# Second attention stage: values' copies ahead of a unit of weights, weights behind the keys' copies, gate row and values' differences at later steps

## The chip, the cores and the metric

The kernel runs on one core of one Trainium2 chip. The time is the device time of one execution in microseconds (us); a kernel's time is the median over its runs. Of the kernel before there are three: 981.32, 981.45 and 982.88 us, median 981.45. One more execution was profiled, and the trace is of that one: it took 983.12 us, of which 981.3 lie between its first and last instruction.

## The reference

Two transformer blocks over 512 tokens of width 1024, all in float32. The first joins a multi-scale pooling branch and a "forgetting" attention. The change lies in the attention of the second block:

```python
h = rmsnorm_2(x, g_norm1[l]) * (1.0 + sc1) + sh1
proj = h @ w_in[l]
q_sb, k_sb, v_sb, q_ca, k_ca, v_ca = jnp.split(proj, split_pts, axis=-1)
o_sb = stick_breaking_attention(hs(q_sb, N_SB_HEADS), hs(k_sb, N_SB_HEADS), hs(v_sb, N_SB_HEADS))
q_ca = rmsnorm_2(hs(q_ca, N_CA_HEADS), g_q[l])
k_ca = rmsnorm_2(hs(k_ca, N_CA_HEADS), g_k[l])
o_ca = chunked_relpos_attention(q_ca, k_ca, hs(v_ca, N_CA_HEADS), rel_bias[l])
mixed = jnp.concatenate([o_sb.reshape(B, S, D_SB), o_ca.reshape(B, S, D_CA)], axis=-1)
x = x + gt1 * (mixed @ w_o[l])
```

`gt1` (the first gate) is a row of 1024 numbers that is needed only in the last line above. Each of the two kinds of attention has 8 heads of width 64.

## The kernel before, in words

Each float32 product is made of three matmuls (lines 2092 to 2094): every factor is split into an upper half in a reduced format (a copy by ScalarE, `wh`, `hh`, `ah`) and the rest (a subtraction by VectorE, `wl`, `hl`, `al`). The weights come in units of 1 MB, loaded by SyncE (line 549) into three buffers `raw`; a load waits until VectorE has taken the last piece of the unit that lay there before (`dve_wl`). ScalarE makes `wh` of it (line 698), VectorE `wl` (line 1237).

The second block's attention is a program of 188 steps. A step is one group of three matmuls of a projection or of the output product; beside it, by a table of numbers (`PACE_S`), stand "beats" of the attention: a score of head h and row block i (S, line 2238), a transposition of the weights of attention (T, line 2259), a product with the values (V, lines 2288 and 2291). Each engine has the same steps written in its own order, and semaphores tie them together. Steps 0 to 63 are the chunked attention's queries and keys, four pairs of heads (pairs 4 to 7); steps 64 to 95 the values of the stick-breaking attention in four row blocks; steps 96 to 159 its queries and keys (pairs 8 to 11); then comes the output product. A pair's heads are 2p and 2p+1: head 8 is scored first at step 33, head 10 at step 49, head 18 at step 137, head 20 at step 154.

SyncE's queue carries, in the order of a loop over m (16 steps each):

- `twice(p)` (line 580): four copies inside SBUF that put a pair's keys, upper and lower half, on the other 64 partitions too, 128 KB each; the first score of the pair waits for all four (`dma_kd0` or `dma_kd1`);
- `table(h)` (line 608): a head's table of position biases, 256 KB;
- the units of weights (line 549), 1 MB;
- for the stick-breaking values: ScalarE writes block i of the values into `values_at(i)` (buffers `rows` and `v_end`, line 1084, at steps 78, 79, 91, 95); `values_out(i)` (line 614) writes it to DRAM as `value_rows`, in two DMAs with runs of 64 numbers (256 bytes); `values_before(i)` (line 624) reads the same rows back, shifted down by one token, into `dv[i]` (named `x` or `sgt` in the trace); a first row of zeros is written by line 648.

VectorE takes the difference of neighbouring values, `dv[i]` less values, at the steps in `DV` (line 1732). ScalarE copies the result's upper half into `v_sb` one step later (`DV_UPPER`, line 1092), VectorE writes the lower half (`DV_LOWER`, line 1736). Nothing reads `v_sb` before step 134 (head 16).

GpSimd's queue has memsets in the tables (line 2045), and between those of heads 9 and 10 the first gate: `gate_rows()` (line 1995) writes the gate from `mod` to DRAM number by number, in two DMAs of 2 KB, and `gate(0)` (line 2002) waits for them and reads the row back to all 128 partitions, 512 KB, into `gt`. It is used by line 1755 from 611.5 us on. After the tables GpSimd clears parts of `v_rows` and `strip` (lines 2057 to 2059) and then waits for the end of the attention.

```python
def score(h, i):
    ...
                else:
                    e.wait_ge(d[f"kd{p % 2}"], 64 * (p // 2) - 64)
```

Of the kernel before, what the change touches and what calls it, by code (L numbers as in the profile page):

```python
# [18 lines left out]
NR, NH = 3, 2  # L19
# [110 lines left out]
def program(nc, x, xcols, wall, wf, poolw, params, fng, wada, crow_in, rel, out):  # L130
# [32 lines left out]
    with ExitStack() as ctx:  # L163
# [331 lines left out]
        TURN_BANK_2 = ((1, 0), (4, 5))  # L495
        VSB_OUT = (78, 79, 91, 95)

        DV, DV_UPPER, DV_LOWER = (87, 88, 113, 122), (88, 89, 114, 123), (89, 90, 115, 124)
        VSB_BANK, W_O_BANK = (0, 1, 2, 0), ((1, 0, 4, 5), (2, 3, 6, 7))

        def o_step(n):
# [43 lines left out]
        def _(e):  # L545
# [5 lines left out]
            def loads_to(last):  # L551
                while todo[0] <= min(last, W_MLP + 3):
                    n = todo[0]
                    todo[0] += 1
                    if n >= NR:
                        e.wait_ge(v["wl"], 4 * (n - NR) + 4)
                    load(n, place[n])
# [52 lines left out]
            def values_out(i):  # L610

                e.wait_ge(a["vsb"], i + 1)
                for odd in range(2):
                    e.dma_start(heads_of(v_mem[1 + 128 * i:129 + 128 * i, :])[:, :, odd, :],
                                values_at(i)[:, :, odd, :]).then_inc(d[f"vm{i % 2}"], 16)
# [14 lines left out]
            for m in range(10):  # L630
                if 1 <= m < 5:
                    twice(3 + m)
                for b_ in range(first_s[16 * m], first_s[16 * m + 16]):
                    x_ = beats_s[b_]
                    if x_ and x_[0] == "S" and x_[2] == 0 and x_[1] + 2 in CA:
                        table(x_[1] + 2)
                if m == 5:
                    values_out(2)
                    values_out(3)
                    values_before(2)  # L640
                    values_before(3)
                loads_to(W_CA + m + 1 + NR)
                if m == 4:
                    for j in range(4):
                        e.wait_ge(d[f"x{4 + j}"], 32)

                    e.wait_ge(g["strip"], 1)
                    e.dma_start(v_mem[0:1, :], dv[0][0:1, :]).then_inc(d["vm0"], 16)
                    values_out(0)
                    values_out(1)  # L650
                    values_before(0)
                    values_before(1)
                if m >= 6:
                    twice(2 + m)
            loads_to(W_O + 1 + NR)
# [1285 lines left out]
        def _(e):  # L1941
# [49 lines left out]
            def gate_rows():  # L1991

                e.wait_ge(v["mod"], 1)
                for c in (0, 4):
                    e.dma_start(gates[0, 128 * c:128 * c + 512].rearrange("(c p) -> p c", p=128),
                                mod[:, 16 + c:20 + c], allow_slow_non_contiguous=True).then_inc(d["g0"], 16)
# [46 lines left out]
            for h in CA:  # L2043
                e.wait_ge(d[f"bt{h % 2}"], 16 * (h // 2 - 3))
                e.memset(bt[h % 2][0:64, 448:512], NEG).then_inc(g["bt"], 1)
                if h == 9:
                    for j in range(4):
                        e.wait_ge(d[f"x{4 + j}"], 32)
                    e.wait_ge(v["tile"], 48)
                    e.memset(dv[0][0:1, :], 0.0).then_inc(g["strip"], 1)  # L2050
                    gate_rows()
                    gate(0)

            e.wait_ge(v["qn"], 8)
            e.wait_ge(v["tile"], 40)
# [1 line left out]
                e.memset(v_rows[i][:, :, 64:128], 0.0).then_inc(g["strip"], 1)  # L2057
            e.memset(strip[:, 0:384], 0.0).then_inc(g["strip"], 1)
            e.tensor_scalar(strip[:, 384:512], ident[:, :], 1.0, None, ALU.mult).then_inc(g["strip"], 1)
            e.wait_ge(t["value"], n_turn(23, 0))  # L2060
            for i in range(4):
                r = sm[:, 144 + i:145 + i]
# [625 lines left out]
```

## Time and profile before

| | |
|---|---|
| median of 3 runs | 981.45 us (981.32, 981.45, 982.88) |
| the profiled execution | 983.12 us |
| its span, first to last instruction | 981.3 us |
| TensorE matmul busy | 959.3 us (98%) |
| VectorE, ScalarE, GpSimd busy | 686.3, 538.6, 83.2 us |
| DMA | 148.69 MB, mean 152 GB/s |
| granted TensorE clock, mean | 0.998 |

A row names the line of the kernel, the engine, the operation with out<-in and the shape, how often it stands there and its time; behind it the engine's idle time and what ended it. A time in us from the start of the span stands in front in the views by time. PE is TensorE, DVE VectorE, ACT ScalarE, POOL GpSimd, SPq SyncE's queue. "DMA to landing" is the time from the issue of a DMA until its data is there.

### The profile page before, as it was taken

The page shows a single profiled execution, that of the slowest core. Times are in us where ns is not written, and L with a number is a line of the kernel's source. Part 1 is how long each engine was busy: PE and PEld are TensorE (multiplying, and loading weights), DVE is VectorE, ACT ScalarE, POOL GpSimd, SP SyncE. Part 2 cuts the span into 40 slices and gives each one's busy share as a digit, 9 for nine tenths or more (in the row PEclk, how much of TensorE's full clock was granted, in tenths as well). Part 3 has the DMA queues.
Part 4 walks back from the last instruction along what each step waited for, and adds up shares of the span by engine and source line. Part 5 has one row for each costly group of instructions (what it writes and reads, how often), then busy time and mean ns, then how long its engine had stood idle before and what let it go on. Part 6 is the DMA issues. An engine that isn't in the chain of part 4 may idle for free.

```text
span 981.3 us, 13125 instructions
## 1 busy us (share of the span) xinstructions
PE 959.3 (98%) x4712; PEld 800.2 (82%) x4712; DVE 686.3 (70%) x1269; ACT 538.6 (55%) x1053; POOL 83.2 (8%) x173
## 2 busy tenths in 40 slices
PE   8999999999999999999989999999999999999998
PEld 7878998878888888777777887788888888888886
DVE  6487888868788759767668886966644853774773
ACT  6448777753223345489877563446645634644520
POOL 4000001011122012100000000110000001000000
PEclk9999999999999999999999999999999999999999
DMA  8205222238787425644433323446777567473201
GB/s 298 82 24 185 66 76 87 81 145 335 298 318 281 173 108 188 241 92 154 111 119 92 102 65 136 158 112 153 180 221 178 171 201 191 115 224 129 85 33 54
DMA packets 36673, 148.69 MB, mean 152 GB/s; under 512 B 9193, under 2 KB 9193, under 8 KB 24706
## 3 DMA queue, kind: packets, MB, share of 16 engines
q1 hardware_dynamic: 23970, 101.41, 29.6%
q0 software_dynamic: 9568, 42.48, 16.5%
q10 hardware_dynamic: 3072, 3.98, 1.2%
q8 instruction: 38, 0.62, 0.3%
q14 instruction: 25, 0.20, 0.1%
HBM read 138.32 MB, written 5.27 MB: 146 GB/s over the span
## 4 chain that ended last, share of the span: by engine, by line
PE 81%; DVE 9%; ACT 4%; DMA 3%; issue 2%; POOL 0%; SPq 0%; ACTq 0%; DVEq 0%; POOLq 0%
PE psum L2092 24%; PE psum L2094 24%; PE psum L2093 24%; PE psum L2259 3%; PE psum L2238 2%; PE psum L2288 1%; DVE wl L1237 1%; PE psum L2291 1%; DMA raw<-in_wall 1%; DVE two L1776 1%; DMA value_rows<-rows 1%; DVE hl L1277 1%; DVE two L1641 1%; DMA al<-al 1%; DVE xt L1273 1%
## 5 line engine op out<-in xcount | busy, mean ns | idle before, releaser
L2092 PE MATMUL psum<-hh,wh 128*128 128x512 f32 (+1 forms) x720 | 274.2, 381 | 0.7 <-DVE hl L1277 0.6
L2094 PE MATMUL psum<-hh,wl 128*128 128x512 f32 (+1 forms) x720 | 267.4, 371 | 0.0
L2093 PE MATMUL psum<-hl,wh 128*128 128x512 f32 (+1 forms) x720 | 267.4, 371 | 0.0
L1237 DVE TENSOR_TENSOR wl<-raw,wh 128x512 fp32r<-128x512 f32 x328 | 213.8, 683 | 45.6 <-ACT wh L698 45.3
L698 ACT ACTIVATE wh<-raw 128x512 fp32r<-128x512 f32 x328 | 188.8, 620 | 84.1 <-PE psum L2094 68.2
L2092 PEld LDWEIGHTS psum<-hh,wh 128*128 128x128 f32 x720 | 135.4, 188 | 24.3 <-DVE hl L1277 1.5
L2094 PEld LDWEIGHTS psum<-hh,wl 128*128 128x128 f32 x720 | 135.3, 188 | 23.7
L2093 PEld LDWEIGHTS psum<-hl,wh 128*128 128x128 f32 x720 | 135.6, 188 | 21.1 <-issue 1.0
L2092 PE MATMUL psum<-wh,ah 128*128 128x512 f32 x224 | 88.5, 395 | 0.0
L2094 PE MATMUL psum<-wh,al 128*128 128x512 f32 x224 | 87.4, 390 | 0.0
L2093 PE MATMUL psum<-wl,ah 128*128 128x512 f32 x224 | 87.3, 390 | 0.0
L857 ACT ACTIVATE pth<-psum 128x128 fp32r<-128x128 f32 (+4 forms) x104 | 45.9, 442 | 16.4 <-PE psum L2259 15.3
L2259 PE MATMUL psum<-ident,p_sb 128*128 128x128 f32 x272 | 47.2, 276 | 7.2 <-DVE ptl L1449 6.8
L1154 ACT ACTIVATE two<-psum 128x512 f32<-128x512 f32 x32 | 19.1, 598 | 62.2 <-PE psum L2094 62.1
L1449 DVE TENSOR_TENSOR ptl<-psum,pth 128x128 fp32r<-128x128 f32 (+1 forms) x96 | 46.2, 482 | 7.4 <-ACT pth L857 6.8
L2092 PEld LDWEIGHTS psum<-wh,ah 128*128 128x128 f32 x224 | 42.1, 188 | 9.2 <-issue 0.6
L2094 PEld LDWEIGHTS psum<-wh,al 128*128 128x128 f32 x224 | 42.1, 188 | 8.9
L2259 PEld LDWEIGHTS psum<-ident,p_sb 128*128 128x128 f32 x272 | 33.5, 141 | 18.7 <-issue 9.3
L2093 PEld LDWEIGHTS psum<-wl,ah 128*128 128x128 f32 x224 | 42.1, 188 | 8.0
L832 ACT ACTIVATE p_sb<-p_sb,sm 128x528 f32<-128x528 f32 (+3 forms) x64 | 36.0, 563 | 9.5 <-DVE sm L1424 8.1
L838 ACT ACTIVATE p_sb<-p_sb,sm 128x528 f32<-128x528 f32 (+3 forms) x64 | 35.7, 558 | 1.5 <-DVE sm L1429 1.4
L2092 PE MATMUL psum<-wh,hh 128*128 128x512 f32 x76 | 31.6, 416 | 1.2 <-DVE wl L1237 1.2
(335 smaller groups left out, 1632.5 us busy)
## 6 DMA issues: line engine op xcount, KB each, us to landing
raw<-in_wall SPq DMA_DIRECT2D x78, 1024.0 KB, 5.1
raw<-in_wall POOLq DMA_DIRECT2D x15, 1024.0 KB, 7.9
wa<-in_wada POOLq DMA_DIRECT2D x24, 512.0 KB, 6.1
gt<-in_wada POOLq DMA_DIRECT2D x20, 512.0 KB, 6.1
xt<-in_xcols SPq DMA_DIRECT2D x8, 264.0 KB, 8.2
cb<-c_rows SPq DMA_DIRECT2D x8, 264.0 KB, 3.2
x<-in_x SPq DMA_DIRECT2D x4, 512.0 KB, 10.1
x_kept<-x SPq DMA_DIRECT2D x4, 512.0 KB, 2.8
```

Of the source, the lines that this page charges most:

```text
L698: e.activation(home(w)[0][:, 512 * c:512 * c + 512], raw_of(w, c), ACT.Copy).then_inc(a["wh"], 1)
L832: e.activation(block_p(h, i), block_p(h, i), ACT.Exp, bias=nmx, scale=1.0 if h in FG else -1.0, accum_out=su).then_inc(a["exp"], 1)
L838: e.activation(block_p(h, i), block_p(h, i), ACT.Copy, scale=mx).then_inc(a["norm"], 1)
L857: e.activation(ph[0:rows, PT[j]:PT[j] + w_], bank[bk][0:rows, 0:w_], ACT.Copy).then_inc(a["turn"], 1)
L1154: e.activation(two[:, n % 2, :], bank[w1_bank(n)], ACT.Relu).then_inc(a["r"], 1)
L1237: e.tensor_tensor(home(w)[1][:, cs], raw_of(w, c), home(w)[0][:, cs].bitcast(F32), ALU.subtract).then_inc(v["wl"], 1)
L1449: e.tensor_tensor(dst, bank[bk][0:rows, 0:w_], ph[0:rows, o:o + w_].bitcast(F32), ALU.subtract).then_inc(v["turn"], 1)
L2092: e.matmul(out_, lh, rh, start=start, stop=False, skip_group_check=True)
L2093: e.matmul(out_, lh, rl, start=False, stop=False, skip_group_check=True)
L2094: return e.matmul(out_, ll, rh, start=False, stop=stop, skip_group_check=True)
L2238: ins = e.matmul(dst[:, size * j:size * j + size], q[:, 128 * i:128 * i + 128], k[:, size * j:size * j + size], start=k is k_up, stop=k is ...
L2259: ins = e.transpose(bank[bk][:, 128 * (i - i0):128 * (i - i0) + 128], head(h)[0][:, o:o + 128], ident[:, :])
```

## The change

```diff
@@ the steps of the values' differences
-        DV, DV_UPPER, DV_LOWER = (87, 88, 113, 122), (88, 89, 114, 123), (89, 90, 115, 124)
+        DV, DV_UPPER, DV_LOWER = (90, 92, 113, 122), (91, 93, 114, 123), (92, 94, 115, 124)
@@ SyncE, in the loop over m
-                loads_to(W_CA + m + 1 + NR)
-                if m == 4:
+                if m == 3:
                     for j in range(4):
                         e.wait_ge(d[f"x{4 + j}"], 32)
 
                     e.wait_ge(g["strip"], 1)
                     e.dma_start(v_mem[0:1, :], dv[0][0:1, :]).then_inc(d["vm0"], 16)
+                if m == 4:
                     values_out(0)
                     values_out(1)
                     values_before(0)
                     values_before(1)
+                if 1 <= m < 5:
+
+                    e.wait_ge(d[f"kd{(3 + m) % 2}"], 64 * ((3 + m) // 2) - 64)
+                loads_to(W_CA + m + 1 + NR)
                 if m >= 6:
                     twice(2 + m)
@@ GpSimd, behind the table of head 9
                     e.memset(dv[0][0:1, :], 0.0).then_inc(g["strip"], 1)
-                    gate_rows()
-                    gate(0)
...
             e.tensor_scalar(strip[:, 384:512], ident[:, :], 1.0, None, ALU.mult).then_inc(g["strip"], 1)
+            e.wait_ge(t["pq"], 12)
+            gate_rows()
+            gate(0)
```

For m from 1 to 4 the unit of weights is now issued only when the pair's four copies have landed, and for m = 4 behind the values' DMAs too. The first gate's three DMAs stand behind GpSimd's last memsets and wait for `pe_pq` 12, the end of step 127.

No instruction is added or removed on an engine. SyncE's queue around m = 4 (L549 is a unit of weights, L580 the keys' copies, L608 a table, L614 and L624 the values to DRAM and back), before:

```order
L580 DMA al<-al 64x512 [waits dve_kl] x2
L608 DMA sgt<-in_rel 128x512 [waits dve_score] x2
L549 DMA raw<-in_wall 128x2048 [waits dve_wl]
L648 DMA value_rows<-x 1x512 [waits dma_x7,dma_x6,pool_strip,dma_x5,dma_x4]
L614 DMA value_rows<-rows 512x1x64 [waits act_vsb]
L614 DMA value_rows<-rows 512x1x64
L614 DMA value_rows<-rows 512x1x64 [waits act_vsb]
L614 DMA value_rows<-rows 512x1x64
L624 DMA x<-value_rows 128x512 [waits dma_vm0]
L624 DMA x<-value_rows 128x512 [waits dma_vm1]
L608 DMA sgt<-in_rel 128x512 [waits dve_score]
```

The same place in the changed kernel:

```order
L580 DMA al<-al 64x512 [waits dve_kl] x2
L608 DMA sgt<-in_rel 128x512 [waits dve_score] x2
L614 DMA value_rows<-rows 512x1x64 [waits act_vsb]
L614 DMA value_rows<-rows 512x1x64
L614 DMA value_rows<-rows 512x1x64 [waits act_vsb]
L614 DMA value_rows<-rows 512x1x64
L624 DMA x<-value_rows 128x512 [waits dma_vm0]
L624 DMA x<-value_rows 128x512 [waits dma_vm1]
L549 DMA raw<-in_wall 128x2048 [waits dve_wl,dma_kd1]
L608 DMA sgt<-in_rel 128x512 [waits dve_score]
```

The unit went from ahead of the values' six DMAs to behind them, with a wait for `dma_kd1`; the row of zeros (L648) moved up to m = 3.

VectorE from step 87 on (L1732 the differences, L1736 their lower halves, L1417 a score's logits, L1449 the lower half of a transposition, L1457 a head's output, L1237 `wl`), before:

```order
L1449 TENSOR_TENSOR ptl<-psum,pth 128x512 [waits act_turn]
L1429 RECIPROCAL sm<-sm 128x1 [waits act_exp] x2
L1732 TENSOR_TENSOR x<-x,rows 128x512 [waits dma_dv0,act_vsb]
L1732 TENSOR_TENSOR x<-x,rows 128x512 [waits dma_dv1,act_vsb]
L1457 TENSOR_TENSOR tmp<-psum,tmp 64x512 [waits dve_ol,act_o]
L1736 TENSOR_TENSOR v_sb<-x,v_sb 128x8x64 [waits act_dv]
L1417 ISA p_sb,sm<-psum,sgt 128x512 [waits pe_turn,pool_bt,pe_score]
L1417 ISA sm 128x1
L1449 TENSOR_TENSOR ptl<-psum,pth 128x128 [waits act_turn]
L1736 TENSOR_TENSOR v_sb<-x,v_sb 128x8x64 [waits act_dv]
L1237 TENSOR_TENSOR wl<-raw,wh 128x512 [waits act_wh]
```

The same place in the changed kernel, whose lines stand four further down (L1736 and L1740 are the differences and their lower halves, L1421, L1453, L1461 and L1241 the rest):

```order
L1461 TENSOR_TENSOR tmp<-psum,tmp 64x512 [waits dve_ol,act_o]
L1421 ISA p_sb,sm<-psum,sgt 128x512 [waits pe_turn,pool_bt,pe_score]
L1421 ISA sm 128x1
L1453 TENSOR_TENSOR ptl<-psum,pth 128x128 [waits act_turn]
L1736 TENSOR_TENSOR x<-x,rows 128x512 [waits dma_dv0,act_vsb]
L1241 TENSOR_TENSOR wl<-raw,wh 128x512 [waits act_wh]
L1421 ISA p_sb,sm<-psum,sgt 128x384 [waits pe_score]
L1421 ISA sm 128x1
L1453 TENSOR_TENSOR ptl<-psum,pth 128x256 [waits act_turn]
L1736 TENSOR_TENSOR x<-x,rows 128x512 [waits dma_dv1,act_vsb]
L1740 TENSOR_TENSOR v_sb<-x,v_sb 128x8x64 [waits act_dv]
L1241 TENSOR_TENSOR wl<-raw,wh 128x512 [waits act_wh]
```

The two differences, which wait for DMAs, stood ahead of head 12's output, head 14's first logits and head 13's first transposition; now these three come first.

## Rows read from the trace of the kernel before

**Rows 1.** Waits of TensorE from 400 to 540 us: total, times, longest

```profile
PE psum L2259 <- DVE ptl L1449: 3.9, 3, 3.0
...
PE psum L2092 <- DVE wl L1237: 1.2, 2, 0.7
```

**Rows 2.** TensorE in order of time: start, us, what, [idle before]

```profile
426.06 0.47 PE L2238 MATMUL psum<-k_sb,q_sb 128*128 128x512 f32 x1 [0.69 <-DMA low<-low]
...
445.89 0.47 PE L2238 MATMUL psum<-ah 128*128 128x512 f32 x1 [1.39 <-DMA al<-al]
...
497.59 0.87 PE L2259 MATMUL psum<-ident,p_sb 128*128 128x128 f32 x3 [3.00 <-DVE ptl L1449]
...
546.15 0.62 PE L2238 MATMUL psum<-v_ca 128*128 128x512 f32 x2
...
566.26 0.47 PE L2238 MATMUL psum<-k_sb,q_sb 128*128 128x512 f32 x1
```

**Rows 3.** Stretches: length, busy PE, PEld, DVE, ACT, POOL, PEclk, DMA share, GB/s

```profile
440.00:480.00 40.00, 37.40 (x187) 29.56 (x186) 29.97 (x82) 36.06 (x86) 0.44 (x3) 1.00 0.39 118
...
494.50:497.50 3.00, 0.09 (x1) 0.00 (x0) 2.75 (x7) 2.58 (x7) 1.96 (x7) 1.00 0.04 14
497.50:501.00 3.50, 3.41 (x10) 2.86 (x11) 3.50 (x9) 3.08 (x8) 0.37 (x1) 0.51 0.31 70
```

**Rows 4.** The chain of waits from 485 to 500 us: start, us, what

```profile
484.77 6.55 DMA value_rows<-rows
...
491.33 3.32 DMA x<-value_rows
```

**Rows 5.** VectorE in order of time

```profile
492.99 0.69 DVE L1732 TENSOR_TENSOR x<-x,rows 128x512 f32<-128x512 f32 x1 [4.16 <-DMA x<-value_rows]
494.75 0.69 DVE L1732 TENSOR_TENSOR x<-x,rows 128x512 f32<-128x512 f32 x1 [1.07 <-DMA x<-value_rows]
```

**Rows 6.** SyncE's queue in order of time

```profile
479.59 0.44 SPq L549 DMA_DIRECT2D raw<-in_wall  x1
480.50 5.37 SPq L614 DMA_DIRECT2D value_rows<-rows  x4
490.22 1.44 SPq L624 DMA_DIRECT2D x<-value_rows  x2
...
536.56 5.38 SPq L580 DMA_DIRECT2D v_ca<-v_ca  x4
...
556.04 1.26 SPq L580 DMA_DIRECT2D low<-low  x2
```

**Rows 7.** Landings: unit of 479.59; value_rows from 484.0; value_rows from 503.3

```profile
DMA to landing us min/median/max: 9.1/9.1/9.1
...
DMA to landing us min/median/max: 4.7/5.6/6.5
...
DMA to landing us min/median/max: 2.1/2.2/2.2
```

**Rows 8.** Landings of keys' copies: from 474.4; 440.6; 421.0 to 423.3; 541.5; from 556.0

```profile
DMA to landing us min/median/max: 2.2/2.2/2.2
...
DMA to landing us min/median/max: 5.0/5.0/5.0
...
DMA to landing us min/median/max: 2.5/2.8/3.6
...
DMA to landing us min/median/max: 2.8/2.8/2.8
...
DMA to landing us min/median/max: 5.6/5.7/5.7
```

**Rows 9.** GpSimd in order of time; last row: landings of L1995's two DMAs

```profile
425.36 0.76 POOL L1995 DMA_DIRECT2D gate_rows<-mod  x1 [7.81 <-issue]
437.85 0.56 POOL L2002 DMA_DIRECT2D gt<-gate_rows  x1 [11.73 <-DMA gate_rows<-mod]
...
DMA to landing us min/median/max: 8.3/10.2/12.2
```

## The prediction

> **What bounds the kernel now.** The table of the page comes first: TensorE's matmuls fill 98% of the span, so only what makes TensorE wait, or run slowly, costs time. Next, the waits of TensorE around the change [rows 1]: between 400 and 540 us it waits 3.9 us for VectorE's lower halves of transpositions, 3.0 of it at once, and 1.2 us for `wl`. TensorE in order of time [rows 2] adds two waits for keys' copies, 0.69 us at 426.06 (head 8's first score) and 1.39 us at 445.89 (head 10's), and places the 3.00 us before 497.59. Then the stretches [rows 3]: in the stretch from 494.5 to 497.5 TensorE is busy 0.09 us, and in the next one, to 501, its granted clock is 0.51, the lower of its two levels (1.2 instead of 2.4 GHz). So TensorE stood still for 3.00 us and then did 3.5 x (1 - 0.51) = 1.7 us less than it could have.
>
> Why does VectorE come late? Its own rows [rows 5]: it stood 4.16 us before the first difference of values (492.99) and 1.07 us before the second (494.75). The transposition that TensorE wanted is behind them in VectorE's order. The chain of waits [rows 4] goes on: the readback behind the second difference took 3.32 us, and before it a write of `value_rows` issued at 484.77 took 6.55 us. In SyncE's queue [rows 6] a 1 MB unit of weights was issued at 479.59, right ahead of the values' writes from 480.50 on. The unit took 9.1 us to land and the writes from 484.0 on 4.7 to 6.5 us; writes of the same kind from 503.3 on, with no unit ahead, took 2.1 to 2.2 us [rows 7].
>
> **The change part by part.** Terms are us of the profiled execution, 983.12 us.
>
> *Values: unit behind them, differences three and four steps later.* Two remedies for one stall. With writes of 2.2 us instead of 6.5, the second block's write, issued at 484.77, lands at 487.0 and not 491.3, its readback (3.32) at 490.3, and the first block's before that. The later place gives more: VectorE, idle from 488.8 until the data came [rows 5], first does head 12's output and head 14's logits, which follow TensorE to step 90. TensorE came to step 91's transposition at 494.59 (497.59 less 3.00, [rows 2]), so it leaves step 90 near 493.5, and the second difference, two steps on, is not wanted before 495. The data are there by 488.7 and 490.3, or, had the landings not improved at all, at 493.0 and 494.7, about when they are wanted. Gain: the 3.00 us, and with them the slow stretch, 1.7 us, since no idle TensorE precedes it: **-4.7**. If VectorE still comes late by a little, the slow stretch goes and some wait stays; bounds -4.7 and 0.
>
> The skill's page "TensorE: Matmul & The Clock Gate" (the Trainium skill, section on the HAM clock gate) says that an idle TensorE falls to half rate, and that the place at which the rate changes varies from run to run. The trace agrees with the first: 3.00 us idle, then 0.51 [rows 3]. By the second, some executions of the kernel before would be spared the 1.7 us.
>
> The times fit that, and this is where I chose. Three runs are 981.32, 981.45 and 982.88, the profiled one 983.12: two values near 981.4 and two near 983.0, apart by 1.6, the price of the slow stretch. I take the median to be executions with the 3.00 us wait but without the slow stretch, and forecast the changed kernel from the profiled execution, whose waits I can see. Against the median the gain is 1.7 us smaller than the sum.
>
> *Cost of the later place.* Four instructions of some 0.6 us each (two differences, 0.69 by their rows, two lower halves of the same shape) enter VectorE's steps 90 to 94, where `wl` of unit 36 and head 14's logits also stand. The same instructions ran before in a row behind the stall, so the work is no more; but in steps 90 to 95 VectorE has little spare time. Nothing reads `v_sb` before step 134, so only what is queued behind matters: `wl`, wanted from step 96, and transpositions. A delay of one such instruction on TensorE, 0.6, is the upper end, nothing the lower; I take **+0.4**. ScalarE's copies (one step behind each difference) move with them at the same count.
>
> *Units behind the keys' copies (m = 1 to 4), gate away from 417 to 443 us.* The copy that head 10's score waited for was issued at 440.6 and took 5.0 us; in the same time ran the gate row's broadcast (issued 437.85 [rows 9]), and behind the copy in SyncE's queue two tables and a unit. Copies with nothing beside them took 2.2 us [rows 8]. The tables stay, the others go: landing before 444, while TensorE was ready at 444.5. The wait of 1.39 goes; ScalarE, busy 36.06 of the next 40 us [rows 3], can follow only as far as it had idle time itself, so I take **-1.2** (bounds -1.39 and 0, if the tables alone delay the copy). For head 8 the last copy took 2.5 of the pair's 2.5 to 3.6 us; at 2.2 it lands 0.3 earlier: **-0.3** (0 to -0.69). The price is that the units come later: by 2 to 3 us for m = 1 to 3, by about 9 for m = 4 (issued near 488). The unit of m = 4 is number 38, which ScalarE first reads at step 113, over 20 steps later, and the others lie as far off, so they cost nothing; for a unit wanted within 5 us of its landing the delay would count in full.
>
> *The gate at its new place.* GpSimd waits for the end of step 127, ten steps ahead of head 18's score at 546.15 [rows 2], so near 535. From there it is 8.6 us to the second write (7.81 + 0.76), 12.5 to the broadcast (425.36 to 437.85, [rows 9]), and about 5 to its landing, so until 561. The row is used from 611.5 on, and GpSimd has nothing queued behind it before that. But it now runs beside the copies of pairs 9 and 10. Pair 9's last copy is issued at 541.5, lands 2.8 later at 544.3 [rows 8] and is wanted at 546.15 [rows 2]: 1.85 us to spare. Pair 8's predecessor at the old place, pair 4, ran beside the gate's writes and took up to 3.6 instead of 2.2, so 1.4 more [rows 8]: still in time. Pair 10's last copies (issue 556.7, 5.7 to land, 562.4) are wanted at 566.26: 3.9 to spare, against some 3 us that a 512 KB broadcast beside them can add (440.6's copy: 5.0 less 2.2). I take **0**, bounds 0 and +1.5.
>
> Sum: -4.7 + 0.4 - 1.2 - 0.3 + 0 = -5.8, with 0.2 for what the 1.2 us of `wl` waits may lose when neighbours move: **-6.0**. 983.12 - 6.0 = **977.1 us**, 4.3 below the median of 981.45. All bounds on the good side give 976.3.
>
> **The rivals.** "Faster" below means more than 0.2% (2.0 us), about what a measurement of this kernel can tell from no change: below 979.5.
>
> *A, part of the wait stays.* VectorE is crowded in steps 90 to 95: behind the stall it was busy 2.75 + 3.50 of 6.5 us [rows 3], to which the first difference, 0.6, is now added. For it: TensorE already waits 1.2 us for `wl` [rows 1]. Against: `wl` is first wanted at step 96, and before the stall VectorE had idle time. It leaves 1.0 to 3.0 of the 3.00 us: 978.1 to 980.1; if the whole wait came back with its slow stretch, 981.8.
>
> *B, the stall was not the copies'.* If the values' small runs (256 bytes) and not the unit make the writes slow, the landings stay at 4.7 to 6.5. Against: the same runs took 2.1 to 2.2 us without a unit. Even then the later steps hide nearly all; waits of 0.5 to 1 us stay: 978.
>
> *C, slower.* The gate's writes delay the keys' copies of pair 9. Price: the gate's own second write took 12.2 us [rows 9]. If the last copy did, it would land at 553.7, and TensorE would wait 7.5 us at 546.15 and then run at the lower clock for another 1.7: 977.1 + 9.2 = 986.3. It decides from a landing over 4.7 us (546.15 - 541.5), and makes the kernel slower than 983.4 (the median and 0.2%) from 9.3 us on (9.3 - 4.65 + 1.7 = 6.3). Against it: 1.4 us was all that the same writes did to pair 4's copies. The Trainium skill's page "DMA: Bandwidth & Descriptors" (Queues, rings and completion order) says that a DMA engine serves its queues in turn, a packet at a time; by that rule GpSimd's small writes would slow SyncE's copies by a share and not hold them for 12 us, but would also slow them wherever the gate is put.
>
> **How the numbers follow.** Forecast (976.0 to 978.2): 0.64. A: 0.18, two thirds of it below 979.5. B, or a small wait at pairs 9 or 10 (978 to 979): 0.08. No measurable change, from a cause that I don't see or from A's full return: 0.06. C: 0.04. Faster 0.64 + 0.12 + 0.08 + 0.02 = 0.86, same 0.10, slower 0.04. The range goes from 975.6 (all bounds, and the `wl` waits gone) to 979.8.
>
> **What would show it.** VectorE: no wait for `value_rows` readbacks, or under 0.5 us. TensorE: no wait of 3.0 us near 491 to 495, and granted clock 1.00 in every stretch. No wait for a copy at heads 8 and 10 over 0.4 us. The values' first writes land in about 2.2 to 3 us. The gate's broadcast lands near 555, and heads 18 and 20 don't wait. A TensorE wait for VectorE of over 1 us in steps 91 to 100 speaks for A, one for a DMA at head 18 or 20 for C. Wrong altogether: the stall goes and the span stays.

## The result, and the profile after

The changed kernel is slower.

| | before | after |
|---|---|---|
| median | 981.38 us (980.17 to 982.88, 4 runs) | 988.31 us (987.84 to 988.78, 4 runs) |
| ratio, 95% interval | | 1.0077 [1.0056, 1.0098] |
| the profiled execution, its span | 983.12, 981.3 us | 988.78, 987.0 us |
| granted TensorE clock, mean | 0.998 | 0.995 |
| forecast | | 977.1 us, range 975.6 to 979.8 |

The measured time lies 8.5 us above the range. In the changed kernel's lines the score's matmuls are L2243, transpositions L2264, lower halves of transpositions L1453, `wl` L1241, the gate's writes L1999 and its broadcast L2006.

First the waits of TensorE, here from 400 to 620 us (total, times, longest), to be held against [rows 1]:

```profile
PE psum L2243 <- DMA v_ca<-v_ca: 11.1, 1, 11.1
PE psum L2264 <- DVE ptl L1453: 2.0, 4, 0.7
PE psum L2097 <- DVE wl L1241: 1.2, 2, 0.7
PE psum L2243 <- DMA low<-low: 0.5, 1, 0.5
```

What was to go is gone: the wait of 3.00 us for `ptl` and the one for `al` (1.39), and head 8's copy costs 0.50 in place of 0.69. At the top stands a new one of 11.1 us, for a copy of keys (L2243 reads them; the program's name for that buffer is `v_ca`). TensorE in order of time places it at head 18's first score, 546.15 before [rows 2]:

```profile
550.70 1.19 PE L2243 MATMUL psum<-v_ca 128*128 128x512 f32 x2 [11.08 <-DMA v_ca<-v_ca]
551.68 0.63 PE L2097 MATMUL psum<-hh,wh 128*128 128x512 f32 x1
552.11 0.63 PE L2098 MATMUL psum<-hl,wh 128*128 128x512 f32 x1
```

Without the wait that score would have stood at 539.62, and before it stood at 546.15: up to there the changed kernel is 6.5 us ahead, and then loses 11.1. The matmuls behind the wait take 0.63 us instead of 0.39. The stretches (length, busy PE, PEld, DVE, ACT, POOL, granted clock, DMA share, GB/s) say why:

```profile
480.00:500.00 20.00, 20.00 (x108) 16.98 (x107) 14.53 (x43) 17.35 (x45) 2.43 (x8) 1.00 0.55 149
...
530.00:532.00 2.00, 1.67 (x12) 1.25 (x10) 1.63 (x4) 1.98 (x6) 0.00 (x0) 1.00 2.36 66
532.00:534.00 2.00, 2.00 (x15) 1.74 (x14) 2.00 (x4) 1.36 (x5) 0.00 (x0) 1.00 0.55 29
...
540.00:542.00 2.00, 0.00 (x0) 0.00 (x0) 0.95 (x3) 0.00 (x0) 0.00 (x0) 1.00 0.86 357
542.00:544.00 2.00, 0.00 (x0) 0.00 (x0) 0.00 (x0) 0.00 (x0) 0.00 (x0) 0.89 1.02 233
...
550.00:552.00 2.00, 1.30 (x3) 1.15 (x4) 0.00 (x0) 0.08 (x1) 0.56 (x1) 0.50 0.21 16
552.00:554.00 2.00, 2.00 (x8) 1.57 (x8) 1.23 (x1) 0.89 (x2) 0.00 (x0) 0.55 0.77 229
```

From 480 to 500, where the stall was, TensorE is busy the whole time at clock 1.00. At head 18 it idles from 539.6 on; the clock falls to 0.50, the lower level, and is still there when the work starts again: 1.3 x 0.50 + 2.0 x 0.45 = about 1.5 us lost.

The DMA column is the second thing to see there: between 530 and 540 the engines are occupied (a packet's time and bytes are counted in the stretch in which it starts, so a share can be over 1), but next to nothing moves; the bytes come from 540 on. What stands in the queues at that time, SyncE's and then GpSimd's, in order of time:

```profile
529.46 0.33 SPq L549 DMA_DIRECT2D raw<-in_wall  x1
529.84 5.38 SPq L580 DMA_DIRECT2D v_ca<-v_ca  x4
```

```profile
528.15 0.85 POOL L1999 DMA_DIRECT2D gate_rows<-mod  x1 [33.53 <-PE psum L2099]
537.96 0.77 POOL L1999 DMA_DIRECT2D gate_rows<-mod  x1 [8.96 <-issue]
550.57 0.56 POOL L2006 DMA_DIRECT2D gt<-gate_rows  x1 [11.85 <-DMA gate_rows<-mod]
```

The gate's first write goes out 1.3 us ahead of a 1 MB unit of weights and 1.7 to 6.6 us ahead of the four copies of pair 9. Their landings, in this order: the unit of 529.46, the copy of 534.76, the gate's two writes:

```profile
DMA to landing us min/median/max: 13.9/13.9/13.9
...
DMA to landing us min/median/max: 15.7/15.7/15.7
...
DMA to landing us min/median/max: 9.4/10.9/12.3
```

Before, the same unit took 5.5 us and the last copy 2.8 [rows 8]. The chain of waits has it as one link: `534.76 15.69 DMA v_ca<-v_ca`. The queues' packets between 529 and 540 us show what kind of slowness it is (packets, MB, share of 16 engines' time):

```profile
q1 hardware_dynamic: 42, 0.34, 90.0%
q0 software_dynamic: 32, 0.00, 1.7%
```

q1 is SyncE's queue: 42 packets in 11 us, 0.90 x 11 x 16 / 42 = 3.8 us each. They are the unit's, 8 KB each (0.34 MB / 42). The experiment with the gate elsewhere (the late gate, below) has the same unit's packets, 8 KB each too, from 529 to 533.8 us:

```profile
q1 hardware_dynamic: 122, 1.00, 64.7%
```

That is 0.647 x 4.8 x 16 / 122 = 0.41 us each. So the unit did not wait behind one long transfer; each of its packets took some nine times as long. q0 is GpSimd's queue: its 32 packets, the gate's first write, took 0.09 us each, and all of them started before 530.4.

The rest of the change, in SyncE's queue, did what it was to do (before: [rows 6]); the last row here is the landing of the four writes:

```profile
478.44 4.78 SPq L614 DMA_DIRECT2D value_rows<-rows  x4
483.27 1.95 SPq L624 DMA_DIRECT2D x<-value_rows  x2
...
DMA to landing us min/median/max: 2.1/2.2/2.3
```

The writes land in 2.1 to 2.3 us instead of up to 6.5, the readbacks are issued at 483.3 instead of 490.2, and VectorE waits for no readback.

So the account of the profiled executions is -6.5 up to head 18, +11.1, +1.5: +6.1, where the spans differ by 5.7. Two questions were left: is the gate's new place alone the cause, and what about it holds the copies?

### The profile page after: what moved, and what is told of

Read it like the earlier page. It is cut to its first block, busy times and chain, and to the rows that moved or that the text cites. A ratio compares the mean times of both kernels' runs of the same rounds, so it can differ in the third digit from the quotient of the medians.

```text
span 987.0 us, 13130 instructions
## 1 busy us (share of the span) xinstructions
PE 959.4 (97%) x4712; PEld 800.4 (81%) x4712; DVE 686.3 (70%) x1269; ACT 538.2 (55%) x1053; POOL 83.2 (8%) x173
## 4 chain that ended last, share of the span: by engine, by line
PE 82%; DVE 9%; ACT 4%; DMA 3%; issue 2%; POOL 0%; ACTq 0%; DVEq 0%; SPq 0%; POOLq 0%
PE psum L2097 24%; PE psum L2099 24%; PE psum L2098 24%; PE psum L2264 3%; PE psum L2243 2%; DMA v_ca<-v_ca 2%; PE psum L2293 1%; PE psum L2296 1%; DVE wl L1241 1%; DMA raw<-in_wall 1%; DVE two L1780 1%; ACT wh L702 1%; DVE hl L1281 1%; DVE two L1645 1%; DVE xt L1277 0%
## 5 line engine op out<-in xcount | busy, mean ns | idle before, releaser
L1241 DVE TENSOR_TENSOR wl<-raw,wh 128x512 fp32r<-128x512 f32 x328 | 214.1, 685 | 45.6 <-ACT wh L702 45.2
L861 ACT ACTIVATE pth<-psum 128x128 fp32r<-128x128 f32 (+4 forms) x104 | 46.1, 444 | 16.2 <-PE psum L2264 15.1
L1453 DVE TENSOR_TENSOR ptl<-psum,pth 128x128 fp32r<-128x128 f32 (+1 forms) x96 | 46.3, 483 | 7.6 <-ACT pth L861 7.1
L2264 PE MATMUL psum<-ident,p_sb 128*128 128x128 f32 x272 | 47.0, 275 | 4.0 <-DVE ptl L1453 3.8
L2264 PEld LDWEIGHTS psum<-ident,p_sb 128*128 128x128 f32 x272 | 33.6, 141 | 15.3 <-issue 5.9
L1442 DVE TENSOR_TENSOR_SCAN p_sb<-p_sb,rows 128x512 f32<-128x512 f32 (+3 forms) x32 | 26.1, 818 | 13.1 <-ACT p_sb L848 13.0
## 6 DMA issues: line engine op xcount, KB each, us to landing
wa<-in_wada POOLq DMA_DIRECT2D x24, 512.0 KB, 5.8
gt<-in_wada POOLq DMA_DIRECT2D x20, 512.0 KB, 7.0
x<-in_x SPq DMA_DIRECT2D x4, 512.0 KB, 10.2
x_kept<-x SPq DMA_DIRECT2D x4, 512.0 KB, 2.8
```

The costliest lines, as they stand in the source:

```text
L861: e.activation(ph[0:rows, PT[j]:PT[j] + w_], bank[bk][0:rows, 0:w_], ACT.Copy).then_inc(a["turn"], 1)
L1241: e.tensor_tensor(home(w)[1][:, cs], raw_of(w, c), home(w)[0][:, cs].bitcast(F32), ALU.subtract).then_inc(v["wl"], 1)
L1442: e.tensor_tensor_scan(p[:, ::-1], p[:, ::-1], ends_at[:, ::-1], 0.0, ALU.mult, ALU.add).then_inc(v["scan_s"], 1)
L1453: e.tensor_tensor(dst, bank[bk][0:rows, 0:w_], ph[0:rows, o:o + w_].bitcast(F32), ALU.subtract).then_inc(v["turn"], 1)
L2264: ins = e.transpose(bank[bk][:, 128 * (i - i0):128 * (i - i0) + 128], head(h)[0][:, o:o + 128], ident[:, :])
```

## The experiments

Theories named in the expectations: **G** is rival C of the prediction, the gate's writes at their new place, and **R** that the rest of the change makes the copies late. Within G, **U** holds that the unit issued between the gate's write and the copies is what carries the delay to them (all in one queue), and **O** that the second write, issued 9 us later, keeps the copies from ending. **U2** and **G2** are told where they are used. Each group of experiments had its own runs of the kernel before beside it (medians 980.66, 979.91 and 981.58 us); ratios are to those.

### Which part costs

**The change without the gate's move.**

```diff
+                    gate_rows()
+                    gate(0)
...
-            e.wait_ge(t["pq"], 12)
-            gate_rows()
-            gate(0)
```

> The changed kernel with the first gate's three DMAs back at their old place (behind the table of head 9). Theory G (the gate's writes at the new place hold back the key copies of pair 9, all the rest of the change gains as forecast): the 11.1 us wait at head 18 and the slow clock behind it are gone, the gain up to step 127 stays except for head 10's copy, which again has the gate's broadcast beside it and may cost 0.5 to 1.4 us; 977 to 978.5 us. Theory R (the moved steps or the units' places are what makes pair 9 late, the gate only stands beside it): the wait at head 18 stays at 8 us or more, 985 to 988 us.

Measured: 976.85 us (976.65 to 977.53, 6 runs), ratio 0.9962 [0.9947, 0.9977], clock 1.000. Head 18 waits for nothing. TensorE's waits from 400 to 620 us:

```profile
PE psum L2263 <- DVE ptl L1453: 2.0, 4, 0.7
PE psum L2096 <- DVE wl L1241: 1.2, 2, 0.7
PE psum L2242 <- DMA low<-low: 0.8, 1, 0.8
```

The rest of the change brings the kernel to the time that the sum gave (977.1 was forecast for the whole). Head 10's copy, which was to lose 0.5 to 1.4 us here with the gate's broadcast beside it again, has no wait. Head 8's has 0.8; more on both below.

**The gate's move alone**, on the kernel before: its three DMAs go behind the memsets with the wait for `pe_pq` 12, nothing else.

> The kernel before with nothing changed but the gate's DMAs, which stand at their new place. Theory G: head 10's copy gains up to 1.4 us, head 18 waits some 11 us more and TensorE runs at the lower clock for a stretch behind it, so slower than before by 9 to 12 us, 990 to 993 us. Theory R: no wait at head 18, 979.5 to 981.5 us.

Measured: 991.75 us (990.68 to 992.17, 4 runs), ratio 1.0110 [1.0087, 1.0133]. The wait is there on its own, and the unit (531.36, behind the gate's 530.06) took 13.6 us:

```profile
PE psum L2239 <- DMA v_ca<-v_ca: 10.4, 1, 10.4
PE psum L2260 <- DVE ptl L1449: 3.7, 5, 1.7
```

The stall before step 91's transposition, for which nothing was changed, is 1.7 us here and not 3.00, and the clock behind it stays at 1.00: its size differs between traces too.

**The later steps alone**: the line with `DV, DV_UPPER, DV_LOWER` of the change.

> The kernel before with only the values' differences at their later steps (90, 92 and what follows them). If the later place alone hides the late data, VectorE waits under 1 us for the readbacks, TensorE's 3.00 us wait and the slow stretch are gone: the profiled execution 4 to 4.7 us below 983.1, so 978.5 to 979 us, and the spread between the runs of a kernel falls. If the data's landing is what counts (the unit ahead of the values' writes), 1 to 3 us of wait stay: 979.5 to 981 us.

**SyncE's edits alone**: the hunk in the loop over m.

> The kernel before with only SyncE's edits (values' DMAs ahead of the unit, units behind the key copies); the differences at steps 87 and 88 and the gate at its old place. If the earlier landing alone does it: the first readback lands about 3 us earlier and VectorE, which is at step 87 at 488.8 us, waits 0 to 1.5 us; TensorE's 3.00 us wait falls under 0.5 and the slow stretch goes, head 8's and 10's waits shrink by 0.3 to 1.0: 977.5 to 979.5 us. If the values' writes are slow by their 256-byte runs, their landings stay at 4.7 to 6.5 us and the wait stays: 980.5 to 981.5 us.

Measured: steps alone 977.65 us (976.64 to 979.77, 7 runs), ratio 0.9968 [0.9954, 0.9983]; SyncE's edits alone 976.80 us (976.09 to 977.50, 6 runs), ratio 0.9960 [0.9945, 0.9974]. Both are faster than I had expected (978.5 to 981 and 977.5 to 979.5), and both together (the first experiment) are no faster than SyncE's alone. They are two cures for one stall. With the steps alone the readbacks go out at 488.40, 10.5 us behind the unit (477.92), as before (490.22 and 479.59), but VectorE has no wait for them. With SyncE's edits alone VectorE keeps one wait, which reaches nobody; its waits from 480 to 500 us:

```profile
DVE p_sb L1421 <- PE psum L2242: 2.5, 2, 1.5
DVE tmp L1461 <- ACT tmp L867: 2.0, 1, 2.0
DVE x L1736 <- DMA x<-value_rows: 1.1, 1, 1.1
```

One thing stands against my reading of head 10's copy: its wait of 1.39 us is absent with the steps alone too, where nothing about that copy was changed. The broadcast ran beside it as before (issued 437.38), and the last copies landed in 2.8 to 2.9 us in place of 5.0.

### What holds the copies

**Copies ahead of the unit**, from m = 6 on, in the changed kernel:

```diff
-                loads_to(W_CA + m + 1 + NR)
                 if m >= 6:
                     twice(2 + m)
+                loads_to(W_CA + m + 1 + NR)
```

> The changed kernel, but from m = 6 on the pair's key copies stand ahead of the unit of weights in SyncE's queue. Theory U (pair 9's copies are late because the 1 MB unit in front of them crawls beside the gate's writes and they are behind it): copies land in 3 to 6 us, the wait at head 18 falls from 11.1 to under 2 us, 976 to 979 us. Theory O (a copy's completion comes only when the gate's writes that are under way have landed, whatever stands in front of it): the last copy still lands with the gate's second write, near 550 us, the wait stays at 9 to 11 us, 986 to 989 us.

Measured: 976.35 us, ratio 0.9971 [0.9946, 0.9997]; nine of ten runs from 976.02 to 976.91, one 986.06. In the profile the copies (issued 528.28, right behind the gate's first write at 528.04) landed in 4.2 to 6.8 us and head 18 waits for nothing; the unit, now issued at 537.16 together with the gate's second write, took 11.6 us, and nobody needs it soon. For U: copies ahead of the unit take about 1 us more than without the gate (below), copies behind it 8 to 10 more. Their packets say the same. From 529 to 532 us, with the gate's write under way, SyncE's queue has these, all of them the copies':

```profile
q1 hardware_dynamic: 160, 0.26, 35.7%
```

That is 0.11 us each, and without the gate beside them (the late gate, below, 533.8 to 540 us) it is 0.10 (342 packets, 35.9%). So a copy inside SBUF is hardly slowed by the write; the unit, which is read from DRAM, is, and a copy behind it in the queue is late with it. The one run of 986 says that it is no safe cure; its execution was not the profiled one, and what happened in it stays open.

**The gate's writes in runs of 16 bytes** instead of 4 (a quarter of the runs; the gate's numbers then land in another order, so this run serves for the time alone):

```diff
-                    e.dma_start(gates[0, 128 * c:128 * c + 512].rearrange("(c p) -> p c", p=128),
-                                mod[:, 16 + c:20 + c], allow_slow_non_contiguous=True).then_inc(d["g0"], 16)
+                    e.dma_start(gates[0, 128 * c:128 * c + 512].rearrange("(p c) -> p c", p=128),
+                                mod[:, 16 + c:20 + c]).then_inc(d["g0"], 16)
```

> The changed kernel with the first gate's two writes in runs of 16 bytes (128 per write) instead of 4 (512 per write); same bytes, same place. The first gate's numbers land in another order, so the output is scaled by a permuted gate. If it is the number of small runs that holds the queues, GpSimd's 9.0 us between the two writes falls to some 2 to 3 us, the landings (9.4, 12.3) to 3 to 5 us, and the wait at head 18 to 0 to 2 us: 976 to 979 us. If any write to DRAM by GpSimd at this place does it, the wait stays near 11 us: 986 to 989 us.

Measured: 977.89 us (977.55 to 979.78, 10 runs), ratio 0.9980 [0.9966, 0.9995]. GpSimd in order of time:

```profile
527.74 1.16 POOL L1999 DMA_DIRECT2D gate_rows<-mod  x2 [32.87 <-PE psum L2099]
530.34 0.54 POOL L2006 DMA_DIRECT2D gt<-gate_rows  x1 [1.45 <-DMA gate_rows<-mod]
```

The same bytes, at the same time, in the same queue: both writes are out in 1.16 us and landed within 2.6, the unit takes 6.9 us, the copies 6.3 to 8.6 (the 512 KB broadcast now runs beside them) and head 18 waits 1.7 us. So it is the small runs that cost, and not the bytes or the place. The edit makes the runs fewer and longer at once and changes the order of the addresses; which of these counts is not separated here.

**The gate behind the last copies** (pair 11's landed), in place of the end of step 127:

```diff
-            e.wait_ge(t["pq"], 12)
+            e.wait_ge(d["kd1"], 256)
```

> The changed kernel with the gate behind the key copies of the last pair (wait for their landing instead of the end of step 127), near 577 us. No key copy is left for it to hold back. Theory G: no wait at head 18, 976 to 977.5 us, if the broadcast lands (577 + 9 + 12.5 + 5 = 603) before its reader near 605 and the unit issued near 589 is not wanted before; each us that either is late adds one, up to 981 us. Theory R: wait at head 18 as before, 986 us or more.

Measured: 976.56 us (976.00 to 976.69, 10 runs), ratio 0.9966 [0.9952, 0.9979]. The writes go out at 574.89 and 583.82, the broadcast at 593.86. The unit of 529.4 takes 5.9 us, the copies 3.2 to 5.8. The packets from 529 to 540 us:

```profile
q1 hardware_dynamic: 464, 1.57, 48.5%
```

This beats both kernels and has the narrowest spread of all, 0.7 us over ten runs; the copies ahead of the unit (976.35) and the gate at its old place (976.85) are as fast within a few tenths. The writes still do harm at their new place: the unit of 588.93, 5.1 us behind the second, takes 9.3 us, but nothing wants it soon.

**One of the two writes left early**: the second half of the gate's row is written at the old place, the first at the new.

```diff
-            def gate_rows():
+            def gate_rows(parts=(0, 4)):
...
+                    gate_rows((4,))
...
-            gate_rows()
+            gate_rows((0,))
```

> The changed kernel with the second half of the gate row written at the old place and the first half at the new one, so only one small-run DMA stands at 528 us (landing near 537.6) and none at 538. Theory O: the last copy (issued 534.8) lands at 538 to 542 instead of 550.5, the wait at head 18 falls from 11.1 to 0 to 3 us, 976 to 980 us. If instead one such DMA is enough to hold the unit and the copies for 14 us, the wait stays above 8 us: 985 to 988 us.

Measured: 986.51 us (986.38 to 987.62, 5 runs), ratio 1.0074 [1.0050, 1.0098]. One write, at 528.69, holds the unit (529.89) for 13.5 us and the copies for 12.2 to 13.7:

```profile
PE psum L2244 <- DMA v_ca<-v_ca: 7.9, 1, 7.9
```

O, by which 976 to 980 us were expected, falls as the main cause: 7.9 of the 11.1 us are there without a second write. The other 3.2 I put down to the second write, from one profile of each: in the changed kernel it landed at 537.96 + 12.3 = 550.3 and the last copy at 550.5.

**The gate a step of projections later:**

```diff
-            e.wait_ge(t["pq"], 12)
+            e.wait_ge(t["pq"], 13)
```

> The changed kernel with the gate eight steps later (end of step 135, near 535 us): the unit issued at 529.5 and the first copies have landed by then, no unit stands within 10 us behind the gate's first write. Theory U2 (what is late is the 1 MB unit issued 1.3 us behind the gate's first write, and the copies behind it in the same queue): unit and copies land in 4 to 6 us, no wait at head 18; the next unit and pair 10's copies (near 548 to 551) stand beside the gate's second write and broadcast and may be late by up to 2 us at head 20: 976 to 979 us. Theory G2 (any key copy beside the gate's writes is held): the copies of 533.3 and 534.8 or those of pair 10 wait for the gate, 5 to 11 us of wait, 983 to 989 us.

Measured: 984.72 us (983.02 to 985.39, 6 runs), ratio 1.0029 [1.0011, 1.0047]. Pair 9 is free (unit 5.9 us, copies 2.9 to 5.6). But the second write now stands 1.0 us ahead of the next unit:

```profile
546.40 0.77 POOL L1999 DMA_DIRECT2D gate_rows<-mod  x1 [8.05 <-issue]
```

The unit of 547.36 took 14.1 us, pair 10's copies behind it 13.3 to 15.6, and TensorE waits at head 20:

```profile
PE psum L2243 <- DMA low<-low: 6.2, 1, 6.2
```

The damage follows the write. It is not something of head 18. Both expectations were wrong in part: by U2 the time was to be 976 to 979, because I had the second write cost at most 2 us at head 20; G2's time is right (983 to 989), and this run alone cannot tell the two, since pair 10's copies stand behind both a write and a unit; `e5_copies_first` can.

**The gate's writes from ScalarE's queue**, at step 127, so that GpSimd has no part in them:

```diff
+                elif n == 127:
+                    e.wait_ge(t["pq"], 12)
+                    e.wait_ge(v["mod"], 1)
+                    for c in (0, 4):
+                        e.dma_start(gates[0, 128 * c:128 * c + 512].rearrange("(c p) -> p c", p=128),
+                                    mod[:, 16 + c:20 + c], allow_slow_non_contiguous=True).then_inc(d["g0"], 16)
...
             e.wait_ge(t["pq"], 12)
-            gate_rows()
             gate(0)
```

> The changed kernel with the gate's two writes issued from ScalarE's queue at step 127 instead of GpSimd's, the broadcast by GpSimd as before. If the small writes to DRAM themselves hold the DMA engines, the unit still lands in 12 to 14 us and head 18 waits 8 to 11 us: 985 to 989 us. If it is the making of 512 descriptors per write in GpSimd's queue (the 9 us between the two writes), the unit lands in 5 to 8 us and head 18 waits 0 to 2 us: 976.5 to 979 us. ScalarE itself loses some 1.6 us at step 127 to the two issues, most of it hidden.

Measured: 985.67 us (985.58 to 986.68, 4 runs), ratio 1.0045 [1.0030, 1.0060]. ScalarE's queue, then GpSimd:

```profile
527.27 0.95 ACTq L1086 DMA_DIRECT2D gate_rows<-mod  x2
```

```profile
537.57 0.58 POOL L2012 DMA_DIRECT2D gt<-gate_rows  x1 [42.84 <-PE psum L2104]
```

Both writes are issued within 1 us and landed by 537.6, earlier than GpSimd's second was even issued. Yet the unit takes 13.9 us, the copies 11.5 to 13.9, and head 18 waits 7.6. So it is not GpSimd's making of the DMA, nor its queue: the transfers themselves hold the others. Two writes 0.5 us apart hold the unit no longer than the one of `e9_half_early` (13.9 and 13.5 us), so the number of small runs alone does not set the length of it, and the wait is that of one write, too (7.6 and 7.9).

**The gate right behind the memsets**, that is the changed kernel without its wait for step 127 (`e.wait_ge(t["pq"], 12)` left out). There the writes fall between 494 and 513 us.

> The changed kernel with the gate right behind GpSimd's memsets, without the wait for step 127: near 494.7 us. Now the last two blocks of values (writes 493.2 to 497.9, readback from 498) and the units of 500 to 512 stand beside its writes. By U2 the values' writes and the unit behind them are held until the first gate write lands near 504; the third difference is wanted at step 113 (near 515), so its readback is just in time: 976 to 979 us. By G2 the readbacks and pair 8's copies (513 to 518) come only with the gate's second write, near 516 to 520: VectorE waits 1 to 5 us, 978 to 983 us.

Measured: 982.46 us (979.09 to 983.18, 10 runs), ratio 1.0005 [0.9989, 1.0021]: the gain is given back. The writes go out at 493.92 and 504.14. The unit issued 1.3 us behind the second, at 505.47, takes 15.1 us and the next one in the queue, of 512.0, 13.3; pair 8's copies behind them take 8.9 to 10.2, and TensorE waits 4.2 us at head 16. The time is G2's (978 to 983), but VectorE, which was to wait, has no wait for a readback; it is again U2's chain of unit and copies, with a price that I had missed. The readback of the last values (505.08, 256 KB from DRAM in packets of 2 KB) took 11.3 us here, and 3.1 us in the changed kernel: small packets are held too when they are read from DRAM. TensorE in order of time:

```profile
526.68 0.77 PE L2242 MATMUL psum<-k_sb,q_sb 128*128 128x512 f32 x1 [4.23 <-DMA low<-low]
```

All places of the gate in the changed kernel, in one table (us; the gate's write named is the last one ahead of the unit that it meets):

| gate | its write, ahead of the unit | unit to landing | copies behind it | wait of TensorE | median |
|---|---|---|---|---|---|
| old place | 425.55, 0.4 | 9.9 | issued ahead of it | none | 976.85 |
| behind the memsets | 504.14, 1.3 | 15.1 (the next 13.3) | 8.9 to 10.2 | 4.2 | 982.46 |
| step 127 (the change) | 528.15, 1.3 | 13.9 | 13.8 to 15.7 | 11.1 | 988.31 |
| one step later | 546.40, 1.0 | 14.1 | 13.3 to 15.6 | 6.2 | 984.72 |
| behind pair 11's copies | none near | 5.9 | 3.2 to 5.8 | none | 976.56 |

The first row is worth a look. At the old place a unit is hit too: with the gate there (`e1_gate_back`) the unit of 425.98 takes 9.9 us, in the changed kernel, without the gate there, the same unit takes 4.7:

```profile
DMA to landing us min/median/max: 9.9/9.9/9.9
```

```profile
DMA to landing us min/median/max: 4.7/4.7/4.7
```

Nobody wants that unit soon, and pair 4's copies are issued ahead of it. So the old place was good for what stood in SyncE's queue there, not because the writes do no harm there.

One number is common to the traces. Cut into half microseconds, the unit's traffic is back above 200 GB/s at 540.0 us in the changed kernel, 541.5 (`e2_gate_only`), 540.5 (`e9_half_early`), 539.5 (`e11_gate_by_scalar`), 558.0 (`e10_gate_a_step_later`), 515.5 (`e8_gate_at_memsets`) and 595.5 (`e7_gate_late`), which is 11.4 to 12.2 us behind the issue of the gate's write ahead of it each time. The kernel before has it too: the unit of 423.93 stood 7.2 us behind the gate's first write (416.75), its traffic came at 428.5, 11.8 us behind that write, and it took 7.2 us in place of 4.7. A unit thus loses what is left of some 12 us when its turn comes. Where a unit stands between both writes the picture is less plain: in `e1_gate_back` most of it moves from 428 to 431 us, and its last packets end at 435.3; in `e5_copies_first` it moves from 538 to 543 us and lands at 548.8, just behind the gate's second write (537.13 + 11.5 = 548.6). With the 16-byte runs of `e6_runs_of_16` traffic is back at 532.5, 4.8 us behind the first write.

## Why the prediction was wrong

**The step that failed** is the gate at its new place, where I wrote "I take **0**, bounds 0 and +1.5". It measured 11.1 of wait and about 1.5 of low clock, 12.6 in place of 0 (by medians 988.31 - 976.85 = 11.5). The upper bound was read from pair 4's copies, which ran beside the same writes at the old place and lost 1.4 us. That row is true and was the wrong neighbour: those copies had no unit of weights between the gate's write and themselves. At the new place SyncE issues the unit first, 1.3 us behind the gate's write, and the copies stand behind it in the same queue. With the copies first (`e5_copies_first`) their loss is indeed of the size I had taken, 1 to 3 us (4.2 to 6.8 against 3.2 to 5.8 with the gate elsewhere, and against pair 4's 2.5 to 3.6), inside the spare time. I looked at what the writes had done to copies and not at what they had done to the unit beside them, which took 7.2 us in the same trace, while its like in front of pair 9 took 5.5. And I used the gate's own second write, 12.2 us [rows 9], to price rival C, where a price of that size belonged inside the bounds of this term, since nothing in the trace excluded it.

**Rival C** had the place, the sign and the culprit, but not the unit between the write and the copies. Its price was low, 7.5 + 1.7 against 11.1 + 1.5, because the last copy took 15.7 us and not the 12.2 that I lent it from the gate's own write; its spare time was about what I had (4.9 from the issue at 534.76 to the demand at 539.62, where I had 4.65). Its chance of 0.04 rested on that single row of another neighbourhood, and was far too small. Beside it stood the Trainium skill's rule in "DMA: Bandwidth & Descriptors" (Queues, rings and completion order) that an engine serves its queues in turn, a packet at a time. The runs don't bear out what I made of it, a slowing by a share: the unit's packets took 3.8 us in place of 0.41, nine times as long, while the copies' packets beside the same write were hardly slowed (0.11 and 0.10 us).

**The values' stall, -4.7**: right for the profiled execution. 3.00 us and the slow stretch are gone. Other executions had less to gain (1.7 us and no slow stretch in `e2_gate_only`). That two cures were in it for one stall was said; that either alone does it (977.65 and 976.80), the runs added.

**The price of the later place, +0.4**: nothing was measured of it. The waits for `ptl` outside the 3.00 us were 5.0 - 3.0 = 2.0 us between 400 and 620 before, and are 2.0 after; those for `wl` are 1.2 both times.

**Head 10's copy, -1.2**: the wait went, but it went in `e3_steps_only` too, whose queues are those of before at that place. So the trace of before showed a wait that comes in some executions only; the edit is not shown to be its cure. **Head 8's copy, -0.3**: 0.19 (0.69 to 0.50). It comes with the gate's leaving and not with the units' later place: the wait is 0.5 us in the seven other traces in which both of the gate's writes have left that place, and 0.7 to 0.9 where one or both are there (`e1_gate_back`, `e3_steps_only`, `e4_sync_only`, `e9_half_early`).

**The sum without the gate**, -6.0: the changed kernel was 6.5 ahead at head 18, and the kernel without the gate's move has a span 6.1 us shorter than before's (975.2 against 981.3). 976.85 against 977.1. Some of this fit is luck: 1.39 us of the 6.1 are head 10's wait, which the edit is not shown to remove, and against the kernel before beside it (median 980.66) the gain is 3.8 us, because that kernel's executions mostly have less of the stall than the profiled one.

**The median of before**: I took 981.4 and 983.0 to be executions without and with the slow clock. Beside the first four experiments thirteen runs of the kernel before lie between 978.73 and 983.18; the five with a mean clock of 0.998 or less lie at 980.94 to 983.18, the six with 1.000 at 978.73 to 980.66. The direction was right, the level not: executions of the kernel before go lower than I thought. SyncE's edits alone, the change without the gate's move, and the gate behind the last copies have spreads of 1.4, 0.9 and 0.7 us, so most of the variation went with the stall; the later steps alone still have 3.1.

**Rivals A and B** did not come: VectorE did not become late by more than 0.7 us at once, and the values' small runs of 256 bytes landed in 2.1 to 2.3 us once the unit was behind them.

What stays open: why a packet of the unit takes 3.8 us behind the small runs, and what sets the 12 us. Traffic came back at 540 us, 2.5 us after the gate's first write had landed (528.15 + 9.4 = 537.5) and long before the second did, so the landing of a write is not the release. The same page of the Trainium skill (Queues, rings and completion order) speaks of turns by packet. The trace doesn't show such turns here: the gate's 32 packets were over by 530.4 us, at 0.09 us each, and the unit's were slow for 10 us after that. Nor did a run separate the number of the small runs from their length or from the order of their addresses.

## What to carry to other kernels

A small transfer in very short runs is to be priced by what any queue loads from DRAM in the next 12 us or so, and not by its bytes: 2 KB in four-byte runs made a 1 MB load of weights late by 8 us, and everything behind the load in its queue with it. Before moving such a transfer, list what each queue issues right after its new place and which of it is wanted soon; a price from its old place is good only if the same things stand behind it there. If a row of the trace shows the moved transfer itself taking 12 us, its neighbours' bound is at least that until something excludes it (here 12.2 us in the trace of before, and then 15.7 for the last copy). And test a bundle of edits in parts: here two parts gained 4 us, either of them nearly all of it alone, and one cost 11; the change with the gate behind the last copies runs in 976.56 us.

## What the runs showed of the hardware that I had not expected

- 2 KB written to DRAM in four-byte runs (512 of them) keeps the 8 KB packets of a load from DRAM in another queue at 3.8 us each (0.41 without), 16 to 66 GB/s for 10 us, and a unit issued 1.0 to 1.7 us behind at 13.5 to 15.1 us whether GpSimd or ScalarE issued the writes (5.5 to 5.9 without). In 16-byte runs, a quarter as many, the unit took 6.9 us.
- The load is free again 11.4 to 12.2 us behind the issue of the write, in eight traces; packets of copies inside SBUF beside the same write take 0.11 us, against 0.10 without it.
- GpSimd's second issue of such a write waits 7.8 to 9.4 us behind the first in every trace with both in its queue; ScalarE issued both within 0.95 us.
- A landing can come well after the last byte: from 546 to 550 us no packet started (0 GB/s), and the copy issued at 534.76 was reported at 550.5, 0.2 us behind the gate's second write; in `e5_copies_first` no packet started from 544 to 548 us either, and the unit landed at 548.8, just behind the second write there.
- Waits come and go between executions: head 10's is 1.39 us in the profile of the kernel before and nothing in `e3_steps_only`, whose queues are the same there, and one run in ten of `e5_copies_first` was 10 us above the rest.
